# A second block's first feed-forward unit, multiplied by tiles of tokens and turned afterwards

## The reference

```python
def second_block(x, positions, w_in, ..., w_ff1, w_ff2, ln2_g, ln2_b):
    for l in range(DEPTH):
        mix = mixer_sublayer(x, positions, w_in[l], ..., w_out[l])
        x = layer_norm_2(DEEPNORM_ALPHA_2 * x + mix, ln1_g[l], ln1_b[l])
        ff = jnp.square(jax.nn.relu(x @ w_ff1[l])) @ w_ff2[l]
        x = layer_norm_2(DEEPNORM_ALPHA_2 * x + ff, ln2_g[l], ln2_b[l])
    return x
```

## Time and profile before

| | us |
|---|---|
| median of 3 runs | 1736.45 (1735.48 to 1736.63) |
| the profiled execution | 1736.08 |
| its span | 1734.8 |
| PE busy | 1666.6 (96%), 11040 instructions |
| DVE busy | 884.8 (51%) |
| ACT busy | 716.3 (41%) |
| POOL busy | 32.6 (2%) |
| mean rate of transfers | 238 GB/s |

### The profile page before, as it was taken

How to read it: one execution, slowest core, us unless ns; L and a number is a source line. 1 busy time by engine, 2 the same in 40 slices (tenths; PEclk the granted TensorE clock), 3 DMA queues, 4 the chain that set the end, 5 groups by cost and what they waited for, 6 DMA issues and landing times.

```text
span 1734.8 us, 25819 instructions
## 1 busy us (share of the span) xinstructions
PE 1666.6 (96%) x11040; PEld 1295.0 (75%) x11040; DVE 884.8 (51%) x1162; ACT 716.3 (41%) x1076; POOL 32.6 (2%) x56
## 2 busy tenths in 40 slices
PE   8899999997999999997999999999999999999998
PEld 7678644433887744433988999889989889989987
DVE  7786411113577611112566656655566575665555
ACT  5685211112575311111554544444446444444443
POOL 0000000000000000000001000000000100000000
PEclk9999999998999999999999999999999999999999
DMA  9336999996725999998645456455556346546552
GB/s 279 111 135 223 374 418 416 416 417 240 217 97 207 371 417 417 417 417 329 196 150 168 146 172 212 158 188 194 195 165 195 106 157 188 211 129 222 187 185 82
DMA packets 193111, 413.12 MB, mean 238 GB/s; under 512 B 16416, under 2 KB 130848, under 8 KB 176608
## 3 DMA queue, kind: packets, MB, share of 16 engines
q1 hardware_dynamic: 191904, 409.83, 65.8%
q10 hardware_dynamic: 1088, 1.57, 0.4%
HBM read 409.54 MB, written 1.84 MB: 237 GB/s over the span
## 4 chain that ended last, share of the span: by engine, by line
PE 84%; DVE 7%; DMA 6%; ACT 2%; issue 1%; POOL 0%; ACTq 0%; SPq 0%; DVEq 0%
PE PS L1603 12%; PE PS L482 10%; PE PS L486 10%; PE PS L483 10%; PE PS L490 8%; PE PS L493 8%; PE PS L494 8%; PE PS L1625 5%; PE PS L509 2%; DMA weights_raw<-in_w_up 2%; DMA arena<-in_w_down 2%; PE PS L1578 2%; DVE weights_lo L462 2%; PE PS L1637 2%; DMA weights_raw<-in_w_in 1%
## 5 line engine op out<-in xcount | busy, mean ns | idle before, releaser
L462 DVE TENSOR_TENSOR weights_lo<-weights_raw,weights_hi 128x1024 fp32r<-128x1024 f32 x368 | 431.4, 1216 | 211.1 <-ACT weights_hi L455 210.6
L482 PE MATMUL PS<-hT_hi,weights_hi 128*128 128x256 f32 (+1 forms) x1488 | 419.7, 282 | 3.8 <-ACT bias L865 2.0
L455 ACT ACTIVATE weights_hi<-weights_raw 128x1024 fp32r<-128x1024 f32 x368 | 365.5, 1044 | 137.1 <-PE PS L494 73.1
L486 PE MATMUL PS<-hT_hi,weights_lo 128*128 128x256 f32 (+1 forms) x1488 | 417.3, 280 | 3.2 <-DVE weights_lo L462 3.2
L483 PE MATMUL PS<-hT_lo,weights_hi 128*128 128x256 f32 (+1 forms) x1488 | 416.8, 280 | 0.0
L482 PEld LDWEIGHTS PS<-hT_hi,weights_hi 128*128 128x128 f32 (+1 forms) x1488 | 280.9, 189 | 10.2 <-issue 6.7
L486 PEld LDWEIGHTS PS<-hT_hi,weights_lo 128*128 128x128 f32 (+1 forms) x1488 | 280.7, 189 | 4.4 <-DVE weights_lo L462 4.4
L483 PEld LDWEIGHTS PS<-hT_lo,weights_hi 128*128 128x128 f32 (+1 forms) x1488 | 280.9, 189 | 1.4
L490 PE MATMUL PS<-weights_hi,opa_hi 128*128 128x512 f32 x384 | 152.6, 397 | 1.3 <-DVE opa_lo L696 1.1
L494 PE MATMUL PS<-weights_hi,opa_lo 128*128 128x512 f32 x384 | 151.9, 396 | 0.0
L493 PE MATMUL PS<-weights_lo,opa_hi 128*128 128x512 f32 x384 | 151.9, 396 | 0.0
(11 more groups left out here) (316 smaller groups left out, 2347.0 us busy)
## 6 DMA issues: line engine op xcount, KB each, us to landing
weights_raw<-in_w_in SPq DMA_DIRECT2D x80, 1024.0 KB, 6.0
weights_raw<-in_w_ff SPq DMA_DIRECT2D x64, 1024.0 KB, 5.3
arena<-in_w_up SPq DMA_DIRECT2D x24, 1024.0 KB, 21.1
arena<-in_w_down SPq DMA_DIRECT2D x24, 1024.0 KB, 16.5
arena<-in_w_gate SPq DMA_DIRECT2D x20, 1024.0 KB, 14.5
weights_at_hi<-in_w_gate SPq DMA_DIRECT2D x18, 1024.0 KB, 19.9
weights_at_lo<-in_w_up SPq DMA_DIRECT2D x18, 1024.0 KB, 18.9
weights_raw<-in_w_down SPq DMA_DIRECT2D x18, 1024.0 KB, 21.1
```

Of the source, the lines that this page charges most:

```text
L455: act.activation(u.flat[0][:, c:e], u.x[:, c:e], ACT.Copy).then_inc(*sig.mark("w_hi", u.u, i))
L462: dve.tensor_tensor(u.flat[1][:, c:e], u.x[:, c:e], u.flat[0][:, c:e].bitcast(F32), ALU.subtract).then_inc(*sig.mark("w_lo", u.u, i))
L482: pe.matmul(o, w[0], x[0], start=start, stop=False)
L486: return pe.matmul(o, w[1], x[0], start=False, stop=stop)
```

## The change

`ff1 0` of each layer is now multiplied by `project_tiles`, which also turns the two tiles of `h`, so `rows_to_T` goes. Its result has tokens on partitions; ACT copies it as it is to `relu_t[1]`, a 128x512 area that is otherwise first written by the relu of `ff1 1`. PE turns the copy with four transposes into another PSUM bank, called `ff1 0 turned`, between the two halves of `ff1 1` (`between=turn_first()`). Relu, square and the two parts then go as before, from that bank. The units 1 to 15 stay as they were.

```diff
--- before.py
+++ after.py
@@ -2121,13 +2121,21 @@
             for i in range(2):
                 pe.wait_ge(*sig.at("merge_dve", n_(f"split {i}")))
                 accumulate_rows(pe, L(f"w_out {2 * i}", f"w_out {2 * i + 1}"), opa, 4 * i, n_("ln1b"), i == 0, i == 1, turns=i == 1)
-            rows_to_T(pe, n_("ln1b"))
-
             banks.turn = 0
-            project_T(pe, L("ff1 0"), hT, "act_took", among=4, norm=n_("ln1b"))
+            project_tiles(pe, L("ff1 0"), hT, "act_took", among=4, norm=n_("ln1b"))
+
+            def turn_first():
+                b = banks.take(pe, n_("ff1 0 turned"), "act_took", among=4)
+                pe.wait_ge(*sig.at("act_took", n_("ff1 0")))
+                for t in range(NT):
+                    for c in range(2):
+                        last = transpose(pe, PS[:, b, c * S + t * P:c * S + (t + 1) * P], relu_t[1][:, t, c * P:(c + 1) * P])
+                last.then_inc(*sig.mark("ps", n_("ff1 0 turned")))
+                yield
+
             for i in range(N_STAGE):
                 if i + 1 < N_STAGE:
-                    project_T(pe, L(f"ff1 {i + 1}"), hT, "act_took", among=4)
+                    project_T(pe, L(f"ff1 {i + 1}"), hT, "act_took", among=4, between=turn_first() if i == 0 else None)
                 if i < N_STAGE - 2:
                     pe.wait_ge(*sig.at("ff_dve", n_(f"up {i}")))
                     accumulate_rows(pe, L(f"ff2 {i}"), opa, 2 * (i % 4), n_("ln2b"), i == 0, False)
@@ -2244,14 +2252,19 @@
             norm_scalar(act, n_("ln1b"))
             feed(n_("w_out 3"))
 
+            up_of = lambda i: n_(f"ff1 {i}" if i else "ff1 0 turned")
             for i in range(N_STAGE + 1):
                 if i < N_STAGE:
                     feed(n_(f"ff1 {i}"))
-                    act.wait_ge(*sig.at("ps", n_(f"ff1 {i}")))
+                    if i == 0:
+                        act.wait_ge(*sig.at("ps", n_("ff1 0")))
+                        copy(relu_t[1], PS[:, banks.of(n_("ff1 0")), :].rearrange("p (t n) -> p t n", t=NT)).then_inc(
+                            *sig.mark("act_took", n_("ff1 0")))
+                    act.wait_ge(*sig.at("ps", up_of(i)))
                     if i > 1:
                         act.wait_ge(*sig.at("ff_dve", n_(f"up {i - 2}")))
-                    act.activation(relu_t[i % 2], one_bank(banks.of(n_(f"ff1 {i}")), 2), ACT.Relu).then_inc(
-                        *sig.mark("act_took", n_(f"ff1 {i}")))
+                    act.activation(relu_t[i % 2], one_bank(banks.of(up_of(i)), 2), ACT.Relu).then_inc(
+                        *sig.mark("act_took", up_of(i)))
                     act.wait_ge(*sig.at("ff_dve", n_(f"square {i}")))
                     if i > 3:
                         act.wait_ge(*sig.at("ps", n_(f"ff2 {i - 4}")))
@@ -2427,7 +2440,7 @@
             for i in range(N_STAGE + 1):
                 if i < N_STAGE:
                     feed(n_(f"ff1 {i}"))
-                    dve.wait_ge(*sig.at("act_took", n_(f"ff1 {i}")))
+                    dve.wait_ge(*sig.at("act_took", n_(f"ff1 {i}" if i else "ff1 0 turned")))
                     dve.tensor_tensor(relu2[i % 2], relu_t[i % 2], relu_t[i % 2], ALU.mult).then_inc(
                         *sig.mark("ff_dve", n_(f"square {i}")))
                     q = 2 * (i % 4)
```

## The result

| | before | changed |
|---|---|---|
| median of 5 runs each | 1735.48 us (1734.81 to 1736.63) | 1726.63 us (1724.64 to 1727.16) |
| ratio, 95% interval | | 0.9947 (0.9932 to 0.9961) |
| profiled execution, its span | 1736.08, 1734.8 | 1726.63, 1725.4 |
| PE busy | 1666.6 | 1663.1 |
| forecast | | 1728.8 (1727.2 to 1732.2) |

The kernel became faster by about half a percent, as forecast, and by more: 8.85 us against 7.6.

What follows compares the result with a forecast made beforehand. The prediction took PE alone to bound the feed-forward part, with a PE wait for tile 1's `h` in each layer's seam ahead. Gains of 9.42 us less costs of 1.8 took 7.6 off 1736.45: 1728.8 us, range 1727.2 to 1732.2.

Steps and rivals of the forecast that it cites:

- U unchanged: Start of tile 1's transposes (U) stays 5.53 us behind the start of tile 0's (T).
- Term 1: 24 matmuls of `ff1 0` move ahead of tile 1's transposes; `ff1 1` begins 4.39 and 5.03 us earlier in the two layers.
- Term 2: At `ff1 1`, PE's first matmul reading the low part comes late, costing 0.22 us a layer.
- Term 3: Four transposes of the result in the middle of `ff1 1` cost PE 0.48 us a layer.
- Term 4: ACT's copy of `ff1 0` ends 1.6 us before PE comes to the transposes, so it costs nothing.
- Term 5: PE waits 0.20 us a layer at `ff2 0`, since relu to low part now follow the transposes.
- The costs together: Waits at `ff1 1` and `ff2 0` plus the four transposes cost 0.90 us a layer, 1.8 for two.
- What is late next: The split of `ff1 2` waits behind the turned bank but keeps three us of slack; the lead is carried to the end.
- (a): Rival: the clock still falls in the seams, 1.6 to 2.3 us per layer, 1730.8 up to 1733 us; chance 0.14.
- (b): Rival: weight supply, from ACT's later start on `ff1 2`, takes back the lead, giving 1736.4 us; chance 0.06.
- (c): Rival: PE stays at 1.2 GHz through half of `ff1 0` and all of `ff1 1`, giving 1742.8 us; chance 0.03.
- (d): Rival: tile 0's rows aren't ready, the 24 matmuls end behind the start of tile 1's transposes, 1732.8 us; chance 0.04.

Runs made afterwards that it cites:

- e3_fillers: The kernel before with 18 instead of 8 fillers between the two turnings behind ln1b, nothing else changed: 1731.15 us, 0.9977 of before.
- e6_square_rows: The changed kernel with ACT taking relu and square of `ff1 0` on the rows ahead of the transposes: 1726.64 us, 0.9947 of before.
- e5_no_fillers: The changed kernel without the four fillers (`keep_clock`) in `project_tiles` of `ff1 0`: 1727.74 us, 0.9957 of before.

## Why the prediction was right and wrong

**The mechanism and the sum of the gain** were right. Point by point, layer 0:

- *U unchanged.* U - T is 5.53 or 5.54 us in every profile.
- *Term 1.* `ff1 1` was to begin at U+5.00; it began at 1096.92, U+5.02, and at U+5.02 in layer 1 too (1538.15 to 1543.17). The parts of the term, moved matmuls and clock, are told apart by `e3_fillers`.
- *Term 2.* 0.22 us forecast; the fourth matmul of `ff1 1` stands at 1097.47 where three steps of 0.117 would put it at 1097.27: 0.20.
- *Term 3.* 0.48 forecast; 0.35 and 0.08 of restart, 0.43. The 275 ns that the Trainium skill gives for one transpose (TensorE: Matmul & The Clock Gate, Part 4: PE-mode transpose) is near the duration of one here, 0.27; four of them cost PE little more than one and a half of that.
- *Term 4.* 1.6 us of cover, cost nothing. The late copy gives 1.65 of cover, and PE does not wait for the copy in the changed kernel.
- *Term 5.* 0.20 forecast; 1103.33 instead of 1103.17, 0.16, and the second matmul 0.10 late (0.34 behind the first, not 0.23): 0.26, which `e6_square_rows` gets back. `ff2 0` at U+11.43, forecast U+11.50.
- *The costs together* come to 0.20 + 0.43 + 0.26 = 0.89 us, where 0.90 was forecast. That they are this near is partly luck: term 3 was taken 0.05 too dear and term 5 0.06 too cheap.
- *What is late next.* Nothing: PE is busy all 158 us behind.
- *Rivals.* (a), (b), (c) and (d) did not come. The Trainium skill (TensorE: Matmul & The Clock Gate, Part 4: PE-mode transpose) holds that transposes do not release the clock; here 8 + 8 + 4 of them stand in the seam at 1.00, and taking away the fillers beside them (`e5_no_fillers`) changed nothing. No run tests whether transposes alone would hold the clock.

**What failed** is the last step, the base and the range. The sum took the stages ahead of T as fixed and allowed "half a us of scatter of runs below"; the three runs shown spread over 1.2 us. The wider sample shows more: 28 runs of the kernel before lie between 1732.28 and 1738.44, with T of layer 0 scattering over 2.1 us in the fourteen profiles and the two seams of before over another 2.1 in sum. No term of the sum covered either scatter.

The miss can be followed in one execution, since the median of the first measurement, 1726.63, is the profiled one. The forecast started from the profiled execution of before, took 7.6 us off and added 0.37 for the median of the three runs. Against it, the 0.37 is not there in this execution; its T is 1.46 us earlier, because the profile of before has the latest T of the four; its seams gained 0.2 more than the 7.6; and 0.2 lie in the rest of the program. These are the 2.2 us between 1728.8 and 1726.63. About two thirds of the miss lie in stages that were not changed.

The base was high as well: 1736.45 is the median of three runs, that of the 28 is 1735.75 (1735.48 beside the first measurement), and 1735.75 less 7.6 gives 1728.15. With a lower end 2.5 us under the forecast both measurements (1726.63 and 1728.03) would have been inside. That the second one came within 0.8 us of the forecast is partly luck: its five executions spread over 5.0 us (1725.78 to 1730.80). Its gain of 7.9 us calls for no further mechanism; the intervals of both, 6.8 to 11.8 us and 4.7 to 9.5 us, hold 7.8.

**The best version** is `e6_square_rows`: it has the shortest seams of all, and with the second matmul of `ff2 0` counted it saves 0.5 us for the kernel in the profile. By runs it is not told apart from the changed kernel.

## What to carry to other kernels

Where PE waits for a norm that comes tile by tile, let the first unit behind it be multiplied with tokens held still, so that the first tile's share runs under the second tile's norm; turning the small result afterwards costs little if it stands half a unit later, when the copy is done (0.43 us for four transposes here; directly behind the unit they cost the seam 1.00 us more). Try first whether more filler work in the wait brings part of the gain, as one changed number did here. Look for a twin of the new order elsewhere in the same trace: here one gave the start of `ff1 1` to 0.02 us. And bound a range by the scatter of the stages that are not changed, which three runs do not show.

## What the runs showed of the hardware

- A wait of 2.7 us of PE, with fillers for 2 us ahead of it, was followed by half-speed matmuls in all ten seams of the order of before that have a profile here (two in each of four profiles of the kernel before, one in each of the two one-layer kernels); their clock reads 0.84 to 0.92 over the whole seam. Both seams of `e5_no_fillers`, with a wait of 1.32 us, read 1.00.
- How long the half speed lasts is not fixed: the same order of work took 19.89 to 21.35 us in the same seam, with 7 to 21 matmuls of `ff1 0` at steps of about 0.21 us.
- A matmul of 256 columns steps by 0.117 us with the weights held still and by 0.119 with the tokens held still (`ff1 1` and `ff1 0` of the changed kernel): it hardly matters which operand is held.
- Four transposes of 128x128 in float32 stand in PE's stream for 0.35 us (changed kernel, layer 0) although each is 0.27 long.
